# An embedding product in halves: 128-row matmuls against pairs of 64-row matmuls in a two-layer decoder trunk

## The reference, cut to what matters

```python
for i in range(DEPTH):                       # DEPTH = 2
    ...
    x = x + rms_norm(f, norm_ffn_post[i])
    ple = rms_norm(p[i] @ w_ple_proj[i], ple_norm[i])   # (512, 256) @ (256, 1024)
    x = x + sigmoid(x @ w_ple_gate[i]) * ple
```

## Time and profile before

| | before |
|---|---|
| time, median of 3 runs | 1235.37 us |
| profiled execution: span from first to last instruction | 1233.0 us |
| median of the runs less that span | 2.4 us |
| TensorE busy | 1226.3 us (99%), 8009 matmuls |
| DVE busy | 839.8 us (68%) |
| ACT busy | 610.8 us (50%) |
| POOL busy | 136.2 us (11%) |

### The profile page before, as it was taken

How to read it: one execution, slowest core, us unless ns; L and a number is a source line. 1 busy time by engine, 2 the same in 40 slices (tenths; PEclk the granted TensorE clock), 3 DMA queues, 4 the chain that set the end, 5 groups by cost and what they waited for, 6 DMA issues and landing times.

```text
span 1233.0 us, 20630 instructions
## 1 busy us (share of the span) xinstructions
PE 1226.3 (99%) x8009; PEld 1128.1 (91%) x8009; DVE 839.8 (68%) x1365; ACT 610.8 (50%) x1156; POOL 136.2 (11%) x209
## 2 busy tenths in 40 slices
PE   9999999999999999999999999999999999999998
PEld 8999888999999998888899999889999999888887
DVE  5675545988888853268976746368888887433788
ACT  7444334555555642237664444264655555322474
POOL 2003531000000000003030036120000000000120
PEclk9999999999999999999999999999999999999999
DMA  7323232233333353320242222322333333444001
GB/s 251 104 65 90 70 103 69 69 102 105 104 103 103 103 188 142 131 69 18 86 122 68 90 65 69 103 77 67 114 104 103 104 103 121 154 154 171 18 18 69
DMA packets 124464, 122.32 MB, mean 99 GB/s; under 512 B 5200, under 2 KB 108752, under 8 KB 124368
## 3 DMA queue, kind: packets, MB, share of 16 engines
q1 hardware_dynamic: 123680, 120.48, 31.0%
q10 hardware_dynamic: 688, 0.53, 0.1%
HBM read 118.90 MB, written 2.10 MB: 98 GB/s over the span
## 4 chain that ended last, share of the span: by engine, by line
PE 98%; DVE 1%; ACT 0%; POOL 0%; issue 0%; DVEq 0%; ACTq 0%
PE bank L993 30%; PE bank L995 30%; PE bank L994 30%; PE bank L1203 2%; PE bank L1262 1%; PE bank L1285 1%; PE bank L1331 1%; PE bank L1283 1%; PE bank L1315 1%; PE bank L1270 0%; PE bank L1307 0%; PE bank L1327 0%; PE bank L1336 0%; PE bank L1213 0%; PE bank L1357 0%; PE bank L1244 0%
## 5 line engine op out<-in xcount | busy, mean ns | idle before, releaser
L993 PE MATMUL bank<-w_hi,h_hi 128*128 128x384 f32 (+2 forms) x564 | 201.2, 357 | 0.6 <-DVE w_lo L1892 0.5
L994 PE MATMUL bank<-w_lo,h_hi 128*128 128x384 f32 (+2 forms) x564 | 194.7, 345 | 0.0
L1890 DVE TENSOR_TENSOR w_lo<-raw,w_hi 128x1024 fp32r<-128x1024 f32 x70 | 83.7, 1234 | 133.7 <-ACT w_hi L1409 133.4
L993 PE MATMUL bank<-h_hi,w_hi 128*128 128x256 f32 x568 | 161.0, 284 | 0.1
L995 PE MATMUL bank<-h_hi,w_lo 128*128 128x256 f32 x568 | 160.7, 283 | 0.0
L994 PE MATMUL bank<-h_lo,w_hi 128*128 128x256 f32 x568 | 160.7, 283 | 0.0
L995 PE MATMUL bank<-w_hi,h_lo 128*128 128x384 f32 (+2 forms) x468 | 157.5, 337 | 0.0
L1409 ACT ACTIVATE w_hi<-raw 128x1024 fp32r<-128x1024 f32 x70 | 70.6, 1053 | 160.6 <-PE bank L995 160.6
L995 PE MATMUL bank<-w_hi,mid_lo 128*128 128x512 f32 x352 | 137.0, 389 | 0.0
L993 PE MATMUL bank<-T_hi,w_hi 128*128 128x256 f32 x448 | 126.8, 283 | 0.0
L994 PE MATMUL bank<-T_lo,w_hi 128*128 128x256 f32 x448 | 126.8, 283 | 0.0
(11 more groups left out here) (296 smaller groups left out, 2942.8 us busy)
## 6 DMA issues: line engine op xcount, KB each, us to landing
raw<-in_w_ffn_in SPq DMA_DIRECT2D x88, 512.0 KB, 3.9
raw<-in_w_ffn_out SPq DMA_DIRECT2D x44, 512.0 KB, 4.2
raw<-in_w_in SPq DMA_DIRECT2D x40, 384.0 KB, 3.8
raw<-in_w_out SPq DMA_DIRECT2D x16, 512.0 KB, 3.8
gw<-in_w_gate SPq DMA_DIRECT2D x16, 512.0 KB, 3.7
raw<-in_w_in SPq DMA_DIRECT2D x10, 512.0 KB, 4.1
raw<-in_w_ple SPq DMA_DIRECT2D x4, 512.0 KB, 6.3
x<-in_x_in SPq DMA_DIRECT2D x3, 512.0 KB, 6.9
```

The lines of the kernel that those rows point to most:

```text
L993: pe.matmul(out_ap, a_hi, b_hi, start=start, stop=False, skip_group_check=True)
L994: pe.matmul(out_ap, a_hi, b_lo, start=False, stop=False, skip_group_check=True)
L1890: last = dve.tensor_tensor(lo, raw[q % RAWS][:, cols], hi, ALU.subtract)
```

## The change

For the embedding product `mm_rows` is replaced by a new function. It cuts each 128-row operand pair into its rows 0 to 63 (`top`) and 64 to 127 (`low`). In a first pass over the six terms (two k times three) the top rows are multiplied for the first 512 output columns and the low rows for the second 512, by turns; in a second pass the top rows serve the second 512 and the low rows the first. Each bank so gets its top and its low part in different passes, and at no time do the two halves write one bank. Between the passes TensorE waits on a semaphore of its own, `halves_swapped`, which the last matmul of the first pass increments. A block has 24 matmuls of 64 rows, 128 stationary and 512 moving columns. The order in which a bank's products are summed changes with it.

```diff
@@ -586,6 +586,7 @@
     swa_o = sem("swa_o")
+    halves_swapped = sem("halves_swapped")
     swa_yr = sem("swa_yr")
@@ -1036,6 +1037,25 @@
+            def mm_halves(a_hi, a_lo, g, m, n):
+
+                top, low = slice(0, HD), slice(HD, P)
+                terms = [(k, a, w) for k in range(2) for a, w in ((a_hi, w_hi), (a_hi, w_lo), (a_lo, w_hi))]
+                for swap in range(2):
+                    if swap:
+                        pe.wait_ge(halves_swapped, n)
+                    for i, (k, a, w) in enumerate(terms):
+                        for half in (1, 0) if swap else (0, 1):
+                            r = low if half ^ swap else top
+                            c = slice(k * D + half * 512, k * D + half * 512 + 512)
+                            half_bank = banks[2 * m + half]
+                            last = pe.matmul(half_bank[:, :], a[r, k, ts(m)], w[slot_of(g)][r, c],
+                                             start=not swap and i == 0, stop=swap == 1 and i == len(terms) - 1,
+                                             skip_group_check=True)
+                    if not swap:
+                        last.then_inc(halves_swapped, 1)
+                return last
+
@@ -1177,7 +1197,7 @@
                     pe.wait_ge(h_lo_ready, h_count(layer, "gate", m))
                     pe.wait_ge(h_copied, layer * TILES + m + 1)
                     pe.wait_ge(p_lo_ready, layer + 1)
-                    last = mm_rows(p_hi, p_lo, 0, g, m, True, True)
+                    last = mm_halves(p_hi, p_lo, g, m, layer * TILES + m + 1)
                 last.then_inc(mm_done, 1)
```

## The result

The kernel after takes 1238.48 us (median of 7 runs, 1238.18 to 1239.07), the kernel before 1235.11 (7 runs, 1234.68 to 1235.66): 3.4 us more, a ratio of 1.0027 with a 95% interval of 1.0016 to 1.0038. Forecast were 3.7 us more and 1239.0 us.

What follows compares the result with a forecast made beforehand. TensorE, busy 99% of a 1233.0 us span, was taken to bound the kernel. Stream 0 plus height changes and swap waits less slack gave 1.83 us a layer, 3.7 in all, so 1239.0 us; range 1237.0 to 1241.5.

Steps and rivals of the forecast that it cites:

- The stream, priced at 0: Embedding product's blocks: twelve pairs take the same 12 x 0.227 us as twelve full matmuls, so 0 added.
- the left-over 0.014: Lower bound on the stream: each pair could lose the 0.014 us beyond its columns' time, 1.3 us gained.
- the offset: Upper bound on the stream: each pair could add the 0.01 us between its halves' starts, 0.7 to 1 us.
- not slower: Rival, chance 0.15: alternating halves hide the left-over in each step, pairs take 0.213 us; 2.4 us more, 1237.8.
- Something shared slows a pair in part: Rival, chance 0.07: a tenth more per pair, 0.023 x 96 = 2.2 us, gives 1241.2.
- Do not run together: Rival, chance 0.08: halves take turns, twelve more steps of 0.227 us a block, 21.8 us in all, 1260.8.
- Changes of height: Switching between 128-row and 64-row work around blocks: 0.19 us in, 0.20 out, 0.15 out to transposes.
- The exchange: TensorE's wait on halves_swapped between a block's two passes: 0.79 us for two steps instead of 0.45, 0.34 lost.
- Slack: TensorE's wait for DVE's ple_n before gate product 1 hides 0.60 us of blocks 2 and 3, nothing of 0 and 1.
- The sum, 3.7 for 3.4: Per layer 1.36 us from blocks 0 and 1 plus 0.47 from blocks 2 and 3, 1.83; two layers, 3.7 us.
- leaves 0.47 us: Blocks 2 and 3 of a layer cost 1.07 us; 0.60 of slack before the gate product leaves 0.47.
- Against its own execution: Profiled span 1233.0 + 3.7 = 1236.7 us; the 2.4 by which the median exceeds the span carried over, giving 1239.0.

Runs made afterwards that it cites:

- the run in turn: Kernel after with all twelve top-row matmuls of a block first, then the wait, then the twelve low-row ones: 1258.86 us in a single run.
- the feed-forward output: Kernel before with strips 1 to 8 of the feed-forward output product in pairs, each second pass behind the next block's first: 1236.19 us against 1235.29.
- the wait-only run: Kernel before, full-height matmuls, with TensorE waiting for its own sixth matmul in each embedding block: 1236.78 us, ratio 1.0013.
- the two half changes: Two kernels against the kernel before: halves only in blocks 0 and 1 of a layer, 1238.22 us; only in blocks 2 and 3, 1235.58 us.

## Why the prediction was right

- **The stream, priced at 0.** Right, and the point on which most hung. Pairs of 512 columns step at 0.227 us, 0.0034 apart. The bounds fall: neither the left-over 0.014 nor the offset shows in the step, so the rival "not slower" falls. The rule that the prediction set beside it, that a weight load overlaps a running matmul only if its row group differs (the Trainium skill, "TensorE: Matmul & The Clock Gate", What overlaps and what doesn't), would on that reading have made pairs step faster than full matmuls, and both step by 0.227. "Something shared slows a pair in part" wanted 0.023 more a pair, and falls by the same step. "Do not run together" is off by the 20 us of the run in turn. The Trainium skill ("TensorEngine Tiling (Array Packing)", Instruction Overhead) gives each matmul some 60 cycles; taken as time on top of every matmul, as the prediction did, these traces do not show it: with 768 pairs in the feed-forward output the step is no longer. The page's own example, a matmul of one column being as long as one of 60, makes it a least duration instead, and matmuls of 512 columns do not test that.
- **Changes of height.** Forecast 0.19 in, 0.20 out, 0.15 out to transposes; measured 0.20, 0.21 (582.28 to 582.95 in the kernel after, less two steps) and 0.16. The entry from transposes was put at 0.19 without a row of its own. It is 0.19: from the last transpose in front of block 2 to the block's second step it is 0.34 us in the kernel before (573.68 to 574.02) and 0.53 in the kernel after (576.03 to 576.57).
- **The exchange.** Forecast 0.34, from the sum of an ACT wait, a wake-up and a cold load; measured 0.34, and 0.33 by itself at full height. That the wait, not the height, sets it, is shown by the wait-only run. How the 0.33 divides into the three parts of that sum was not measured beyond the 0.44 to 0.45 us until the load.
- **Slack.** That 0.60 of blocks 2 and 3 is hidden before the gate product and nothing of blocks 0 and 1 is shown by the two half changes.
- **The sum, 3.7 for 3.4.** Two terms were mis-sized and partly cancel. A layer's blocks cost 1.94 instead of 1.83 (1.44 instead of 1.36 for blocks 0 and 1, 0.50 instead of 0.47 left over by blocks 2 and 3). The height changes are 0.04 of that. The rest fits this: the first steps after a restart, that is after a wait or a change of height, are longer (567.91 to 568.84 is four steps in 0.93 us, 0.2325 each, 0.02 more in all), and there are five restarts more in a layer. And "leaves 0.47 us" of blocks 2 and 3 was taken as final for both layers; in layer 0 another 0.48 came back in two waits for DVE 30 us later. The rule I had used at the gate product, that DVE's chain does not shift with TensorE, holds there too (`kept` is not moved by blocks 2 and 3), and I stopped asking after the first wait.
- **Against its own execution.** The 2.4 us between span and median were carried over. For the profiled execution of the kernel after its own time is known: 1239.07 for a span of 1237.3, so 1.8 lie around it; the other 0.6 was that one execution compared with a median. The difference of 3.7 us was added to a median of runs, so this does not touch the forecast.

## What to carry to other kernels

Here, splitting the array in rows gave nothing, because the contraction fills it: two halves side by side stream as one full matmul does, and what was added is about 0.2 us at each change of height and 0.33 us at each wait of TensorE for itself. The wait cost nothing where a pass of other matmuls stood between. Price a delay by what runs beside it, and follow it past the first wait that it fills: the next wait for the same engine can give back more. And when work is moved ahead to fill a wait, ask what it will itself wait for.
